# Two-layer transformer with 64 experts on one Trainium2 core: the expert loop taken unit by unit, with a weight ring of five slots and a divided late copy

## The reference

```python
def swiglu(t, wg, wu, wd):
    return (jax.nn.silu(t @ wg) * (t @ wu)) @ wd
...
def moe_ffn(h, router_w, router_bias, w_gate, w_up, w_down, s_gate, s_up, s_down):
    top_idx, top_w = route(h, router_w, router_bias)        # 8 of 64 experts for each token
    order = jnp.argsort(e)                                   # assignments sorted by expert
    ...
    yb = lax.map(lambda a: swiglu(a[0], w_gate[a[1]], w_up[a[1]], w_down[a[1]]), (xb, blk_exp))
    ...
    return swiglu(h, s_gate, s_up, s_down) + routed
```

## Time and profile before

| | us |
|---|---|
| median of three runs | 3734.99 |
| the profiled execution's own time | 3724.67 |
| its span on the core | 3722.9 |
| TensorE busy, share of the span | 3094.3, 83% |
| VectorE busy | 1427.8, 38% |
| ScalarE busy | 820.8, 22% |
| expert loop of layer 0, from the first gate/up matmul to the last down matmul | 984.6 to 1897.8 |
| expert loop of layer 1 | 2772.0 to 3652.0 |

### The profile page before, as it was taken

One profiled execution on the slowest core, in us unless ns is written; L12 is line 12 of the kernel. 1 busy time (PEld: TensorE's weight loads), 2 busy tenths in 40 slices (PEclk: granted clock), 3 DMA queues, 4 the chain that ended last, 5 costly groups with the idle time before them and its releaser, 6 DMA issues. The chain is left out here.

```text
span 3722.9 us, 63767 instructions
## 1 busy us (share of the span) xinstructions
PE 3094.3 (83%) x24444; PEld 1636.1 (44%) x24445; DVE 1427.8 (38%) x2720; ACT 820.8 (22%) x1688; POOL 558.3 (15%) x534
## 2 busy tenths in 40 slices
PE   7998989889889888798888989899887766666686
PEld 4555669845433333233324546698442222222232
DVE  3434534454433333333355436344442222222235
ACT  2323432222111111111133325322221110001112
POOL 0100034210111111011142100241210000000014
PEclk8998989999999999899998999999998888878898
DMA  9103310133368866777775104101257586777666
GB/s 385 68 9 118 134 45 4 60 122 147 142 264 320 322 270 249 317 283 315 312 275 202 45 7 159 38 4 60 105 198 293 231 346 268 300 303 298 282 243 236
DMA packets 133669, 724.16 MB, mean 195 GB/s; under 512 B 24801, under 2 KB 42721, under 8 KB 96737
## 3 DMA queue, kind: packets, MB, share of 16 engines
q1 hardware_dynamic: 84800, 544.14, 37.2%
q0 software_dynamic: 28224, 102.77, 7.9%
q10 hardware_dynamic: 20448, 74.46, 4.9%
HBM read 619.62 MB, written 101.71 MB: 194 GB/s over the span
## 5 line engine op out<-in xcount | busy, mean ns | idle before, releaser
L2274 PE MATMUL psum<-arena 128*64 x1792 | 867.5, 641 | 399.1 <-issue 204.7
L2276 PE MATMUL psum<-arena 128*64 128x512 f32 x1792 | 868.3, 641 | 0.0
L2274 PEld LDWEIGHTS psum<-arena 128*64 128x64 f32 x1792 | 254.0, 148 | 955.3 <-issue 955.3
L2376 DVE COPY arena<-arena 128x4096 f32 x116 | 266.4, 2297 | 555.8 <-DMA arena<-in_w_dn 551.1
L2252 POOL DMA_INDIRECT arena<-h,arena x112 | 184.0, 1643 | 1582.3 <-PE psum L2265 1558.7
L826 PE MATMUL psum<-arena 128*128 128x480 f32 (+3 forms) x1088 | 403.6, 528 | 14.2 <-PEq L164 6.9
L2290 PE MATMUL psum<-arena 128*64 128x512 f32 x896 | 396.6, 595 | 0.0
L2288 PE MATMUL psum<-arena 128*64 x896 | 396.5, 595 | 0.0
L826 PEld LDWEIGHTS psum<-arena 128*128 128x128 f32 x1088 | 208.0, 194 | 188.5 <-issue 176.6
L2343 ACT ACTIVATE arena<-psum 128x256 f32<-128x256 f32 x112 | 43.1, 384 | 1072.6 <-PE psum L2276 1072.6
L2276 PEld LDWEIGHTS psum<-arena 128*64 128x64 f32 x1792 | 253.5, 147 | 0.0
(11 more groups left out here) (360 smaller groups left out, 4193.7 us busy)
## 6 DMA issues: line engine op xcount, KB each, us to landing
arena<-in_w_gu SPq DMA_DIRECT2D x130, 2048.0 KB, 11.7
arena<-in_w_dn SPq DMA_DIRECT2D x130, 1024.0 KB, 14.8
y_slots<-arena ACTq DMA_DIRECT2D x122, 512.0 KB, 11.0
arena<-in_ada SPq DMA_DIRECT2D x24, 2048.0 KB, 7.7
y_slots<-arena SPq DMA_DIRECT2D x4, 4096.0 KB, 27.5
arena<-in_w_gdn SPq DMA_DIRECT2D x6, 1536.0 KB, 10.1
arena<-in_w_out SPq DMA_DIRECT2D x2, 4096.0 KB, 14.2
arena<-in_w_tok SPq DMA_DIRECT2D x4, 1920.0 KB, 7.7
```

The costliest lines, as they stand in the source:

```text
L2274: nc.tensor.matmul(psum[half(0), 2 + r, :], xT[:, r, rows_of(k, 0)], W[:, bass.ds(slot + k * 2 * DE, 2 * DE)], start=(k == 0), stop=(k == ...
L2276: last = nc.tensor.matmul(psum[half(1), 2 + r, :], xT[:, r, rows_of(k, 1)], late_gu[r][:, k * 2 * DE:(k + 1) * 2 * DE], start=(k == 0), st ...
L2376: nc.vector.tensor_copy(late_gu[r][:, :], W[:, bass.ds(slot, GU)]).then_inc(lgu_ready, 1)
```

## The change

The loop goes from unit to unit: behind a prologue of two units, each step u is turn(u+2), turn_hidden(u), gate_up(u+1), down(u). A pass of the hardware loop still has two steps. `WRING` becomes 5, in SBUF that other tiles held: there is now one `late_gu` and one `late_dn`, and `W_top` lies above the ring as it was; the tail phase still loads three experts (`LOW`). The slot of an expert is now its number modulo 5, worked out with a multiplication by 205 and a shift by 10. The gate/up copy of the late half is in two parts: VectorE copies k 0 to 3, ScalarE k 4 to 7, each behind its own wait for the weights; TensorE waits for the second part between k 3 and k 4. TensorE itself no longer waits for the weights. `blocks_done` is now `units_done`. The PSUM banks of the outputs, three before, become two (LEFT and RIGHT), and the hidden rows of both parities share one place.

```diff
-WRING = 4
+WRING = 5
+LOW = 3
...
-                        ch(V.tensor_copy(qi[:, :], bf[:, 0:NBC]))
-                        ch(V.tensor_scalar(qi[:, :], qi[:, :], WRING - 1, None, ALU.bitwise_and))
-                        ch(V.tensor_copy(bf[:, 0:NBC], qi[:, :]))
+                        ch(V.tensor_scalar(fifth[:, :], bf[:, 0:NBC], 205.0, None, ALU.mult))
+                        ch(V.tensor_copy(qi[:, :], fifth[:, :]))
+                        ch(V.tensor_scalar(qi[:, :], qi[:, :], 10, None, ALU.logical_shift_right))
+                        ch(V.tensor_copy(fifth[:, :], qi[:, :]))
+                        ch(V.scalar_tensor_tensor(out=bf[:, 0:NBC], in0=fifth[:, :], scalar=-float(WRING), in1=bf[:, 0:NBC], op0=ALU.mult, op1=ALU.add))
...
-                        ch(V.tensor_scalar(bf[:, T_FREE:T_FREE + NE], ends[0:1, :], 3.0, None, ALU.add))
-                        ch(V.tensor_copy(bf[:, T_END - 1:T_END], bf[:, T_FREE + NE - 1:T_FREE + NE]))
+                        ch(V.tensor_scalar(bf[:, T_FREE:T_FREE + NE], ends[0:1, :], HALVES - 1.0, None, ALU.add))
+                        ch(V.tensor_scalar(bf[:, T_END - 1:T_END], ends[0:1, NE - 1:NE], -1.0, None, ALU.add))
...
+                sbuf(st, "W_top", [P, (WRING - LOW - 1) * WSLOT], place=w0 + (LOW + 1) * WSLOT)
                 GU, DN = DK * 2 * DE, 2 * D
-                late_gu = [sbuf(st, f"late_gu{r}", [P, GU]) for r in range(2)]
-                late_dn = [sbuf(st, f"late_dn{r}", [P, DN]) for r in range(2)]
+                late_gu = sbuf(st, "late_gu", [P, GU])
+                late_dn = sbuf(st, "late_dn", [P, DN])
...
-                                free = sp.value_load(plan[0:1, T_FREE + e - WRING:T_FREE + e - WRING + 1], min_val=1, max_val=NU + 1)
-                                sp.wait_ge(blocks_done, free)
+                                free = sp.value_load(plan[0:1, T_FREE + e - WRING:T_FREE + e - WRING + 1], min_val=1, max_val=NU)
+                                sp.wait_ge(units_done, free)
...
+                        def gate_up(u, r, at):
+                            pe.wait_ge(lg_ready, u + 1)
+                            pe.wait_ge(xT_ready, u + 1)
                             for k in range(DK):
...
+                        def turn_hidden(u, r):
+                            pe.wait_ge(hid_ready, u + 1)
+                            if not (isinstance(u, int) and u == 0):
+                                pe.wait_ge(hT_ready, u)
...
+                        def down(u, r, at):
+                            pe.wait_ge(hT_ready, u + 1)
+                            pe.wait_ge(ldn_ready, u + 1)
+                            for n, bank, free, sem in ((0, LEFT, ys_ready, left_done), (1, RIGHT, yv_ready, units_done)):
+                                if not (isinstance(u, int) and u == 0):
+                                    pe.wait_ge(free, u)
...
+                        later = later_pairs(pe)
+                        first = [slot(pe, u, 0) for u in range(2)]
+                        gate_up(0, 0, first[0])
+                        turn(2, 0, 32)
+                        turn_hidden(0, 0)
+                        gate_up(1, 1, first[1])
+                        down(0, 0, first[0])
+                        with pe.Fori(0, NU // 2 - 1) as i:
+                            with pe.If(later > i):
+                                at = [slot(pe, 2 * i + 1 + r, 0) for r in range(3)]
                                 for r in range(2):
-                                    b = 2 * i + r
-                                    wait_weights(pe, need[r])
-                                    pe.wait_ge(lgu_ready, b + 1)
-                                    pe.wait_ge(xT_ready, b + 1)
-                                    pe.wait_ge(hid_ready, b + 1)
-                                    gate_up(r, slot[r])
-                                    if r == 1:
-                                        pe.wait_ge(hid_ready, b + 2)
-                                        pe.wait_ge(hT_ready, b)
-                                        turn_hidden(0)
-                                    pe.wait_ge(gathered[r], 16 * i + 32)
-                                    pe.wait_ge(xT_ready, b + 2)
-                                    turn(r)
-                                pe.wait_ge(hid_ready, 2 * i + 4)
-                                turn_hidden(1)
-                                pe.wait_ge(hT_ready, 2 * i + 2)
-                                pe.wait_ge(yv_ready, 2 * i + 1)
-                                pe.wait_ge(ldn_ready, 2 * i + 1)
-                                down(0, 0, slot[0], left_done)
-                                down(0, 1, slot[0], blocks_done)
-                                pe.wait_ge(hT_ready, 2 * i + 3)
-                                pe.wait_ge(ys_ready, 2 * i + 1)
-                                pe.wait_ge(ldn_ready, 2 * i + 2)
-                                down(1, 0, slot[1], left_done)
-                                pe.wait_ge(ys_ready, 2 * i + 2)
-                                down(1, 1, slot[1], blocks_done)
+                                    turn(2 * i + r + 3, 1 - r, 16 * i + 32 + 16 * r)
+                                    turn_hidden(2 * i + r + 1, 1 - r)
+                                    gate_up(2 * i + r + 2, r, at[r + 1])
+                                    down(2 * i + r + 1, 1 - r, at[r])
+                        pe.wait_ge(gathered[0], 16 * later + 32)
+                        pe.wait_ge(gathered[1], 16 * later + 32)
+                        turn_hidden(2 * later + 1, 1)
+                        down(2 * later + 1, 1, slot(pe, 2 * later + 1, 0))
...
+                        def copy_gu(need, at):
+                            for r in range(2):
+                                act.wait_ge(w_in[r], need[r])
+                            nc.scalar.copy(late_gu[:, GU // 2:GU], W[:, bass.ds(at + GU // 2, GU // 2)]).then_inc(lu_ready, 1)
...
+                                at = [slot(act, 2 * i + 3 + r, 1) for r in range(2)]
+                                need = [weights(act, 2 * i + 3 + r) for r in range(2)]
                                 for r in range(2):
-                                    b = 2 * i + r
...
+                                    take_x(2 * i + r + 3, 1 - r)
+                                    gate(2 * i + r + 2, r)
+                                    copy_gu(need[r], at[r])
+                                    send(2 * i + r + 1, 1 - r, 16 * i + 16 + 16 * r)
...
+                        later = later_pairs(dve)
+                        early = [slot(dve, u, 1) for u in range(3)]
+                        need = [weights(dve, u) for u in range(3)]
+                        copy_gu(need[0], early[0])
                         for i in range(NLT):
                             token_weights(ch, i, wk, route_keep)
-                        pairs = used_pairs(dve)
-                        with dve.Fori(0, NU // 2) as i:
-                            with dve.If(pairs > i):
-                                late = [late_block(i + 1, r) for r in range(2)]
+                        copy_dn(early[0])
+                        product(0, 0)
+                        copy_gu(need[1], early[1])
+                        take_hidden(0, 0)
+                        product(1, 1)
+                        copy_gu(need[2], early[2])
+                        right(0, 0, 16)
+                        with dve.Fori(0, NU // 2 - 1) as i:
+                            with dve.If(later > i):
+                                at = [slot(dve, 2 * i + 1 + r, 1) for r in range(4)]
+                                need = [weights(dve, 2 * i + 3 + r) for r in range(2)]
                                 for r in range(2):
...
+                                    take_hidden(2 * i + r + 1, 1 - r)
+                                    copy_dn(at[r])
+                                    product(2 * i + r + 2, r)
+                                    copy_gu(need[r], at[r + 2])
+                                    right(2 * i + r + 1, 1 - r, 16 * i + 16 + 16 * r)
+                        take_hidden(2 * later + 1, 1)
+                        copy_dn(slot(dve, 2 * later + 1, 1))
+                        right(2 * later + 1, 1, 16 * later + 16)```

How the instructions stand now, beside how they stood. VectorE, one pass of the loop, before (L2394 silu times up, L2396 hidden rows, L2376 late gate/up, L2405 right half, L2379 late down):

```order
L2394 TENSOR_TENSOR arena<-arena,psum 128x256
L2396 COPY arena<-psum 128x256
L2376 ISA
L2376 COPY arena<-arena 128x4096
L2404 ISA
L2405 COPY arena<-psum 128x512
L2379 ISA
L2379 COPY arena<-arena 128x2048
L2403 REGISTER_ALU
L2405 COPY arena<-psum 128x512
```

More of the change, by code:

```diff
@@ L2246, in _, with gather, turn @@
                     def _(pool):
-                        pairs = used_pairs(pool)
-                        def gather(b):
-                            if b >= 4:
-                                pool.wait_ge(turned, b - 3)
```

(48 more changed lines are left out.)

155 lines of the change are left out of this document (66 added, 89 removed).

## The result

The changed kernel takes **3475.55 us**, the median of 4 runs (3471.45 to 3476.64), against 3734.53 for the kernel before (3728.97 to 3739.82): a ratio of 0.9305, with a 95% interval of 0.9289 to 0.9321. The profiled execution took 3474.74 us.

A forecast was written before the change was run, and what follows sets the result against it. Neither TensorE nor DMA fills either loop; seam, weight waits and clock leave 158 and 314 us to win. Layer 0 780 (133 less), layer 1 802 (78 less), minus 5: 206 off 3734.99, said 3530 us, range 3480 to 3635.

The forecast's parts named there:

- Prices: Waits for weights in the expert loops: needed load lands in 13.5 us, between 10.2 and 15.3, plus SyncE 0.4, landing-to-matmul 1.4.
- nine units without slack: Layer 1 units whose load is released by the down just ahead: 14.0 us each, 15.8 with clock, 142 us together.
- twenty with one unit of slack: Layer 1 units with one unit of work between release and need: ten with two new experts 50 us, ten others 22.
- VectorE's reads: Eight table reads by VectorE in each pass: 0.3 us for each pair, 9 us in layer 0, 7 in layer 1.
- the DMA's own rate takes some back: Low end of the range: landing 10.2 saves 80 us, part lost to the DMA's rate, giving 3490.
- The rival that the fifth slot does nothing: SyncE still waits for expert e-2 ahead of each load, so the loop runs with four slots: 3820 us, chance 0.04.
- The seam: TensorE's 1.78 us idle between hardware-loop passes: taken as gone with three fewer reads; rival that it stays: 3610 to 3640, chance 0.15.
- the late copy in two parts: Late gate/up copy: VectorE's half 1.22 us, ScalarE's about 1.87, nothing on the path unless weights are late.
- the clock: Lower granted clock in gate_up behind a weight wait: 1.8 us on each of nine units, 9 us on others.
- late loads: Layer 0: 10 us for three units with one unit of slack and loads later than their median.
- the 5 that I took off for the starts: Taken off the gain: 1 us for the five-slot table, 4 because part of the start lies ahead of the windows.
- The rule: Skill page's HBM bound of about 358 GB/s: an expert would take 8.8 us, some 40 us less won; trace disagrees.

The follow-up runs named there:

- ring four: The changed kernel with a ring of four slots instead of five, order by unit kept: 3767.21 us, ratio 1.0107 against the kernel before.
- the run with one expert behind: Changed kernel with separate gate/up and down semaphores, gate/up space released at gate_up's end, ScalarE's down wait after its left-half copy, down loads one expert behind: 3357.16 us.

## Why the prediction was right and wrong

**What failed.** The mechanism was forecast rightly and the time was too high by 54 us. The step that failed is the sizing of the waits for weights under *Prices*: a landing of 13.5 us, chosen between 10.2 and 15.3, for each of nine units without slack (14.0 us of waiting), and 72 us for the twenty with one unit of slack, five of them with both experts going out together. The runs showed a landing of 11.8 us and nine waits of 11.8 to 12.2 for the first, and 53 us with two such units for the second: 37 us less than the sum had. Beside it stand 16 us of VectorE's reads, which cost about nothing. The low end of the range failed with it. By the prediction's own count a landing of 10.2 saves 80 us, which is 3450; it went back up to 3490, and 3480 in the end, because "the DMA's own rate takes some back", and no row gave that term a size. In the profile after, layer 1's loop moves 316 GB/s at a DMA share of 0.79, so the rate was not yet the bound.

**Right: what bounds the loops, and the sign.** Release by unit together with the fifth slot gave the gain; the order with ring four gains 87 us in layer 0 and loses 131 in layer 1. The fifth slot with the old order was not tried. The rival that the fifth slot does nothing, at 3820, is ruled out by the result; ring four measures what it would have cost, 3767. The seam does not stay, and nothing got slower.

**Right: the late copy in two parts.** 1223 ns on VectorE (L2389) and 1894 on ScalarE (L2356), against 1.22 and about 1.87. The page after:

```profile
L2356 ACT COPY arena<-arena 128x2048 f32 x114 | 215.9, 1894 | 249.8 <-DMA arena<-in_w_dn 238.8
L2389 DVE COPY arena<-arena 128x2048 f32 x114 | 139.5, 1223 | 254.6 <-DMA arena<-in_w_dn 226.9
```

**Right in kind, wrong in size: the landing.** The nine units without slack were found: nine waits of 11.8 to 12.2 us stand in layer 1. Each was priced at 14.0, and they sum to 107.6 us for 126, 18 less. Some 15 of these are the landing of 11.8 for 13.5. The other 3 are SyncE: the load goes out 0.1 us behind the down (2728.02), where 0.4 was taken. The median of 15.3 was of loads in a burst, with another expert ahead of them, and here that expert goes out behind.

**Too dear: the twenty units with one unit of slack.** They stood at 50 + 22 = 72 us. All waits of gate_up but the nine and the start's 9.9 sum to 170.6 - 107.6 - 9.9 = 53. Two of them, 10.27 and 9.97 us, are the case where both experts of a unit go out together (priced at 9.6): for the second, the loads go out at 3081.91 and 3083.37, and the later one is there at 3103.6, 20 us after its issue. I took half of the ten for that case, and it was two. One more of 0.8 is at the loop's start. The other twelve are 1.3 to 4.5 us, 2.7 in the mean, for the 2.2 of the sum, but they are twelve and not the eighteen that would be left. The loads behind these twelve landed 12.9 to 18.1 us after their issue, by VectorE's copy that starts with them. So one landing for all was wrong both ways: 13.5 was too long for the units without slack, and a little short here. What held these loads was not taken apart.

**Too cheap: the clock.** I put 1.8 us on each of nine and 9 in all on others, 25. In 18 gate_ups of layer 1, each behind a wait, the length is 8.3 to 9.6 us for 7.0, and the sum of what is over is 33.

**Too dear: VectorE's reads.** 9 us in layer 0 and 7 in layer 1 were put down to eight reads at the top of a pass. Layer 0's waits on the late copy are 14.3 us in all, of them 10.7 ahead of its first gate_up, and the loop's step is 11.8 us: about nothing of it is on the path. In layer 1 every wait behind the start ends with a copy that itself waited for the landing of weights, so there the reads are on no wait's path either.

**The seam went, but the price of a read was off.** The step said that three reads fewer are 2.2 us and so more than the seam of 1.78. With six reads the new order shows 1.05, and the loop is 0.75 us longer a pass, so three reads are worth about 1 us on TensorE and not 2.2, and the reads are not all of the 1.78. What the other 0.7 was, no run here tells. It did not come back in the new order, and that the seam is gone was so far luck.

**The sums.** Layer 1: 802 - 18 (no slack) - 19 (one unit of slack) - 7 (reads) + 8 (clock) = 766, measured 770. Layer 0: 755 + 6 + 4 = 765, as I had 10 us for late loads and 4 came; measured 771.5, and TensorE alone is busy for 758.8. The loops are 9 and 32 us of the 54 by which the forecast was high, and 3 are of the 5 that I took off for the starts. The last 10 are in how the forecast was set: the profiled execution was 10.3 us below its median before and 0.8 after, and the sum, worked out from the profile, was taken off the median. By the two profiled executions the change won 250 us and not 259. So the 4.5 us between the result and the range are less than this offset and are chance; the 37 us of the waits are not.

**The rule.** The Trainium skill, "DMA: Bandwidth & Descriptors", section "Where 436 GB/s comes from", puts the bound of transfers from HBM at about 358 GB/s for a core. In the run with one expert behind, layer 1's loop moves 374 GB/s over 652 us, stores and gathers among them, and 424 over 472 us of it. So for this kernel, which runs on one core alone, the measurement disagrees, and the 40 us were rightly not taken.

## What to carry to other kernels

Price a wait for weights by the load that is needed, not by the median of a burst, and each class of waits by its own loads: from its issue to its last byte, with what travels beside it; here 11.8 us without slack, of which 3.5 were a part that the waiting instruction does not read and 1.5 a gather that could come later. Before moving a release, count for each unit how much work lies between it and the need; that count (nine without slack with five slots, 24 with four) was found again wait by wait in both kernels. Then give each consumer its own semaphore and release each part of a buffer when its own last reader is done: that made 3475.6 us into 3357.2 with the same engines and the same bytes. Then look at the DMA share slice by slice: once it is full for most of a loop, as here at 424 GB/s, a better order of the same loads has little left to win there.

## What the hardware showed that was not expected

- Order alone moved 133 us: the down parts three experts behind the gate/up parts gave 3505.8 us, two behind 3373.1. Layer 0's loop, where gate_up hardly waits, went from 774.7 to 833.5 us with it. There ScalarE waited 169.7 us for down weights, for 9.6 with two behind, and SyncE's queue 607.5 us for gate_ups, for 545.6. Which of these sets the pace was not taken apart.
- The length of a wait does not by itself tell what the clock costs behind it. Behind the nine waits of 11.8 to 12.2 us gate_up took 8.3 to 9.6 us. Two waits of nearly the same length, 3.58 and 3.96 us, were followed by a gate_up of 6.9 us at a granted clock of 1.00 and by one of 9.3 at 0.74:

```profile
2795.91 0.64 PE L2287 MATMUL psum<-arena 128*64 x1 [3.58 <-DVE arena L2389]
2802.83 0.59 PE L2309 MATMUL psum<-arena 128*64 x1
...
3000.75 1.11 PE L2287 MATMUL psum<-arena 128*64 x1 [3.96 <-DVE arena L2389]
...
3010.06 0.59 PE L2309 MATMUL psum<-arena 128*64 x1
```

So the 1.8 us of the earlier trace rows was one size of several. Behind the wait of 11.97 us the granted clock was 0.64 in the first 7 us, thus for most of them at 1.2 GHz.
- Three more reads of a table by TensorE made a seam of 1.05 us in each pass and the loop of layer 0 0.75 us longer a pass, where VectorE's seven take about 5 us with the loop's start. Whether a read is cheaper on TensorE or partly hidden there, no run tells.
